# HGRN2 and dilated-attention block: the first projection's input is loaded a second time, turned by the host, and scaled in place

## The chip, the cores and the metric
The kernel runs on one core of one Trainium2 chip. The metric is the device time of one execution in microseconds (us). All times below are those of the kernel before the change, unless a text says otherwise.

## The reference
Everything is float32. `x` has 2048 tokens (rows) of 1024 features. Only the first lines matter here; the mixers that follow are unchanged.

```
u    = x * rsqrt(mean(x*x, axis=-1) + 1e-6) * norm_w      # one factor per token, one gain per feature
proj = u @ w_in                                          # 1024 x 4096
hg_q, hg_f, hg_i, hg_z, at_q, at_k, at_v, at_z = split(proj)
o_hg = per-head RMSNorm of an HGRN2 gated recurrence (4 heads), times silu(hg_z)
o_at = mix of three dilated causal window attentions (8 heads), times silu(at_z)
out  = rms_norm(x + concat(o_hg, o_at) @ w_out, final_norm_w)
```

## The kernel before
The program is written engine by engine; each engine runs its own instructions strictly in the order written, and semaphores order them across engines. The 2048 tokens are 16 **tiles** of 128 tokens. Every projection is made of three matmuls in a reduced-precision fp32 form: `u` and the weights are each split into a high and a low part (`u_hi`, `u_lo`, `w_hi`, `w_lo`), so that `u_hi`*`w_hi` + `u_hi`*`w_lo` + `u_lo`*`w_hi` is accumulated over the eight 128-feature slices (lines 665 to 667). The stages are: a **prologue** that makes `u_hi` and `u_lo` for all 16 tiles and, on the way, the values and gates of the first head from them; the HGRN2 heads; the attention units; the output projection and the last norm. `u_hi` and `u_lo` stay in SBUF for all the projections.

The matmul contracts over the partitions, so `u` must lie *turned*: features in the partitions, tokens along a row. `x` arrives with tokens in the partitions. In the prologue each tile t goes through this:

- SyncE loads the tile's 128 x 1024 floats of `x` into one of four slots `xt` (`load_x`, line 431), 0.5 MB each.
- ScalarE squares it and sums along the row (line 1106; signals `xsq_done`). GpSimd makes the token's inverse norm `rstd` of the sum, in two tiny instructions (lines 1321, 1325; `rstd_done`).
- VectorE multiplies the tile by `rstd`, one number per partition (line 1498; `xn_done`).
- TensorE turns the product in eight 128 x 128 transposes into two PSUM banks (`x_transposes`, line 699; `xT_done`).
- VectorE multiplies the two banks by the gains `norm_w` into a buffer `un` (line 1471, 128x512 twice; `un_done`).
- ScalarE copies `un` to `u_hi` (line 1101; `uhi_done`); VectorE subtracts to get `u_lo` (line 1471, 128x1024; `ulo_done`).
- TensorE runs the tile's 24 matmuls (`phase1_tile`, lines 665 to 667; `vz_ready`). ScalarE copies the result to `vg_tile` and takes a sigmoid of the gate half (lines 1091, 1092; `sig_done`). GpSimd multiplies twice (lines 1305, 1307; `gated`). SyncE stores the tile to DRAM (`phase1_store`, line 420).

In the order that is written out by hand, TensorE turns tile t+2 just before the matmuls of tile t, ScalarE squares tile s in its step s and handles the result of tile s-4 in the same step, and SyncE, in its step s, first stores tile s-5 and then loads tile s+4 of `x`. That load waits for `xn_done`, since line 1498 is the last reader of the slot. SyncE waits in this same order, so whatever stands behind a wait stands still with it:

```
for step in range(TILES + 5):
    if step >= 5:
        phase1_store(0, step - 5)
    if step - 3 in SPLIT_AT:
        load_piece(1, SPLIT_AT.index(step - 3))
    if step + X_SLOTS < TILES:
        after(xn_done, step + 1)
        load_x(step + X_SLOTS)
```

Four times in the prologue (after tiles 1, 4, 7 and 10, `SPLIT_AT`), a piece of the next weights is loaded and split too. TensorE runs 28 and then 12 idle transposes of the identity (line 706) before the first tiles are ready. After tile 15 the first `queries` (lines 665 to 667, now 128x512) wait for `sig_done` of tile 15.

Of the kernel before, what the change touches and what calls it, by code (L numbers as in the profile page):

```python
# [25 lines left out]
X_SLOTS = 4  # L26
Q_SLOTS = 3
# [103 lines left out]
def build(nc, x, w_groups, w_units, w_out, norm_w, gate_g, lb_logits, final_w, rope, near_mask, far_mask, tri_masks, out):  # L131
# [7 lines left out]
    with ExitStack() as ctx:  # L139
# [70 lines left out]
        ss, rstd = p2.take(TILES), p2.take(TILES)  # L210

# [80 lines left out]
        rstd_done, xn_done, xT_done = sem("rstd_done"), sem("xn_done"), sem("xT_done")  # L292
# [105 lines left out]
        def _(sp):  # L398
# [33 lines left out]

            load_x(0)
# [225 lines left out]
        def _(pe):  # L659
# [34 lines left out]
            def x_transposes(t):  # L694
                pe.wait_ge(xn_done, t + 1)
                if t >= 2:
                    pe.wait_ge(un_done, t - 1)
                for k in range(KT_N):
                    last = nc.tensor.transpose(bank[1 + 2 * (t % 2) + k // 4][:, (k % 4) * P:(k % 4 + 1) * P],
                                               xn[t % 2][:, k * P:(k + 1) * P], ident[:, :])  # L700
                last.then_inc(xT_done, 1)
# [6 lines left out]
            idle_transposes(28)  # L708
            x_transposes(0)
            idle_transposes(12)  # L710
            x_transposes(1)
# [1209 lines left out]
```

## Time and profile before

| | us |
|---|---|
| median of 3 runs | 1281.92 (1281.78 to 1283.44) |
| profiled execution, its own time | 1279.88 |
| its span in the profile | 1278.1 |
| TensorE matmuls busy | 1244.5 (97%) |
| VectorE busy | 704.9 (55%) |
| ScalarE busy | 461.2 (36%) |
| GpSimd busy | 434.4 (34%) |
| first matmul of tile 0 | 15.34 from the span's start |
| first matmul of the first `queries` (end of the prologue) | 80.32 |

In the rows further down, PE is TensorE, PEld its weight load, DVE VectorE, ACT ScalarE, POOL GpSimd and SP SyncE; SPq is SyncE issuing a DMA. A row of the order of time gives the start, how long it took, engine, line and operation, what is written and read, and how many instructions were merged; in brackets stands how long the engine had been idle, and what released it. `room` is the work area of SBUF in which `xt`, `xn`, `un`, `rstd` and others lie. Durations overlap a little in a pipelined engine, so where a step is costed the starts are compared.

### The profile page before, as it was taken

The page shows a single profiled execution, that of the slowest core. Times are in us where ns is not written, and L with a number is a line of the kernel's source. Part 1 is how long each engine was busy: PE and PEld are TensorE (multiplying, and loading weights), DVE is VectorE, ACT ScalarE, POOL GpSimd, SP SyncE. Part 2 cuts the span into 40 slices and gives each one's busy share as a digit, 9 for nine tenths or more (in the row PEclk, how much of TensorE's full clock was granted, in tenths as well). Part 3 has the DMA queues.
Part 4 walks back from the last instruction along what each step waited for, and adds up shares of the span by engine and source line. Part 5 has one row for each costly group of instructions (what it writes and reads, how often), then busy time and mean ns, then how long its engine had stood idle before and what let it go on. Part 6 is the DMA issues. An engine that isn't in the chain of part 4 may idle for free.

```text
span 1278.1 us, 24337 instructions
## 1 busy us (share of the span) xinstructions
PE 1244.5 (97%) x8944; PEld 1086.7 (85%) x8944; DVE 704.9 (55%) x1933; ACT 461.2 (36%) x1328; POOL 434.4 (34%) x441
## 2 busy tenths in 40 slices
PE   7999999999999999999999999999999998999997
PEld 6988989999999989999888888888888876888886
DVE  6837867887767797111455445545554455333232
ACT  6631222222222212112555455545554556421121
POOL 5543344243534413121243335334533334021000
PEclk9999999999999999999999999999999999999999
DMA  6520122211221222241455455545554666544431
GB/s 231 158 91 18 55 63 83 75 59 59 63 79 59 75 67 75 77 127 57 119 143 139 121 138 140 144 119 141 149 139 120 165 178 201 161 140 148 148 116 66
DMA packets 121717, 143.94 MB, mean 113 GB/s; under 512 B 20352, under 2 KB 86400, under 8 KB 121600
## 3 DMA queue, kind: packets, MB, share of 16 engines
q1 hardware_dynamic: 117024, 134.26, 37.1%
q10 hardware_dynamic: 4576, 8.13, 2.3%
q8 instruction: 72, 1.18, 0.4%
q14 instruction: 45, 0.37, 0.1%
HBM read 87.56 MB, written 29.62 MB: 92 GB/s over the span
## 4 chain that ended last, share of the span: by engine, by line
PE 56%; DMA 4%; DVE 2%; POOL 1%; ACT 1%; issue 1%; SPq 1%; POOLq 0%; ACTq 0%; DVEq 0%
PE bank L836 6%; PE bank L835 6%; PE bank L834 6%; PE bank L862 5%; PE bank L864 5%; PE bank L863 5%; PE bank L926 3%; PE bank L935 3%; PE bank L990 3%; PE bank L997 3%; PE bank L665 2%; PE bank L666 2%; PE bank L667 2%; PE bank L963 2%; PE bank L971 1%; PE bank L979 1%
## 5 line engine op out<-in xcount | busy, mean ns | idle before, releaser
L665 PE MATMUL bank<-w_hi,u_hi 128*128 128x256 f32 x768 | 220.8, 287 | 2.9 <-DVE u_lo L1471 2.4
L666 PE MATMUL bank<-w_lo,u_hi 128*128 128x256 f32 x768 | 217.9, 284 | 0.0
L667 PE MATMUL bank<-w_hi,u_lo 128*128 128x256 f32 x768 | 217.8, 284 | 0.0
L665 PEld LDWEIGHTS bank<-w_hi,u_hi 128*128 128x128 f32 x768 | 147.9, 193 | 4.6 <-DVE u_lo L1471 3.9
L666 PEld LDWEIGHTS bank<-w_lo,u_hi 128*128 128x128 f32 x768 | 147.9, 193 | 0.1
L667 PEld LDWEIGHTS bank<-w_hi,u_lo 128*128 128x128 f32 x768 | 147.8, 192 | 0.0
L1471 DVE TENSOR_TENSOR room<-room 128x256 f32<-128x256 f32 (+6 forms) x386 | 131.1, 387 | 16.6 <-POOL room L1356 10.7
L834 PE MATMUL bank<-u_hi,w_hi 128*128 128x512 f32 x256 | 107.8, 421 | 0.6 <-issue 0.5
L1471 DVE TENSOR_TENSOR t<-bank,tab 128x512 f32<-128x512 f32 x64 | 42.5, 684 | 118.2 <-DMA tab<-in_rope 53.5
L835 PE MATMUL bank<-u_lo,w_hi 128*128 128x512 f32 x256 | 101.9, 398 | 2.8 <-DMA far_v<-values 2.8
L1385 POOL TENSOR_TENSOR r<-t,t 64x512 f32<-64x512 f32 x16 | 35.0, 2187 | 199.6 <-DVE w L1758 188.8
L862 PE MATMUL bank<-u_hi,mT_hi 128*128 128x512 f32 x256 | 102.0, 398 | 0.7 <-DVE mT_lo L1471 0.6
L836 PE MATMUL bank<-u_hi,w_lo 128*128 128x512 f32 x256 | 102.0, 398 | 0.0
L665 PE MATMUL bank<-u_hi,w_hi 128*128 128x512 f32 x256 | 101.0, 395 | 0.6 <-ACT sg_tile L1092 0.6
L864 PE MATMUL bank<-u_hi,mT_lo 128*128 128x512 f32 x256 | 100.0, 391 | 0.0
L667 PE MATMUL bank<-u_hi,w_lo 128*128 128x512 f32 x256 | 99.8, 390 | 0.0
L863 PE MATMUL bank<-u_lo,mT_hi 128*128 128x512 f32 x256 | 99.8, 390 | 0.0
L666 PE MATMUL bank<-u_lo,w_hi 128*128 128x512 f32 x256 | 99.7, 390 | 0.0
L1186 ACT COPY pT<-bank 128x512 f32<-128x512 f32 x60 | 35.3, 588 | 130.3 <-PE bank L963 130.3
L1471 DVE TENSOR_TENSOR hh<-bank,xr 128x512 f32<-128x512 f32 x32 | 22.1, 690 | 107.0 <-PE bank L864 103.2
L935 PEld LDWEIGHTS bank<-ks,qd 128*128 128x128 f32 x256 | 78.5, 310 | 1.7
L935 PE MATMUL bank<-ks,qd 128*128 128x128 f32 (+3 forms) x256 | 79.8, 319 | 0.0
(169 smaller groups left out, 2840.9 us busy)
## 6 DMA issues: line engine op xcount, KB each, us to landing
qd<-turned SPq DMA_DIRECT2D x64, 256.0 KB, 4.5
stage<-in_w_groups SPq DMA_DIRECT2D x42, 256.0 KB, 4.0
room<-in_x SPq DMA_DIRECT2D x16, 512.0 KB, 4.0
values_gates<-vg_tile SPq DMA_DIRECT2D x64, 128.0 KB, 1.7
room<-values_gates SPq DMA_DIRECT2D x16, 512.0 KB, 3.9
tab<-in_rope SPq DMA_DIRECT2D x16, 512.0 KB, 4.4
wide<-mix_weights SPq DMA_DIRECT2D x32, 256.0 KB, 3.9
xr<-in_x SPq DMA_DIRECT2D x16, 512.0 KB, 4.8
```

Source lines behind the costliest of these rows:

```text
L665: yield nc.tensor.matmul(dst, lhs_hi(k), rhs_hi(k), start=(k == 0), stop=False)
L666: yield nc.tensor.matmul(dst, lhs_hi(k), rhs_lo(k), start=False, stop=False)
L667: last = nc.tensor.matmul(dst, lhs_lo(k), rhs_hi(k), start=False, stop=(k == KT_N - 1))
L834: yield nc.tensor.matmul(bk[:, :], wh[:, k, :], u_hi[:, k, sl], start=(k == 0), stop=False)
L835: yield nc.tensor.matmul(bk[:, :], wh[:, k, :], u_lo[:, k, sl], start=False, stop=False)
L836: last = nc.tensor.matmul(bk[:, :], wl[:, k, :], u_hi[:, k, sl], start=False, stop=(k == KT_N - 1))
L862: yield nc.tensor.matmul(bk[:, :], mT_hi[t % 2][:, k, :], wo_hi[half][:, k, :], start=(k == 0), stop=False)
L863: yield nc.tensor.matmul(bk[:, :], mT_hi[t % 2][:, k, :], wo_lo[half][:, k, :], start=False, stop=False)
L864: last = nc.tensor.matmul(bk[:, :], mT_lo[t % 2][:, k, :], wo_hi[half][:, k, :], start=False, stop=(k == KT_N - 1))
L926: last = nc.tensor.matmul(dst, q[h][:, z, j * P:(j + 1) * P], key_tiles(h, T), start=(z == 0), stop=(z == 1))
L935: last = nc.tensor.matmul(bank[2 + h][:, 0:P * (g + 1)], q[h][:, z, j::CH], keys, start=(z == 0), stop=(z == 1))
L1471: return nc.vector.tensor_tensor(dst, a_, b_, op)
```

## The change
The host gives `x` a second time as `x_turned`: for each tile, features in the partitions, tokens along the row. A tile of it goes straight to the buffer `xT`, which has three slots of two tiles each (a **pair**, 1 MB). The `x` in token order is still loaded, for the squares alone. TensorE no longer turns `x`; it turns a column of `rstd` that is broadcast along the row, one 128 x 128 transpose per tile, which leaves the 128 inverse norms in a row in every partition (`rstd_rows`). VectorE then makes `xT * norm_w * rstd` in place, one instruction per 128-feature slice for both tiles of a pair (`scaled`). Tiles 0 and 1 are handled one by one. `u_hi` and `u_lo` are made from `xT`. The order of the work is written anew on all engines. In the new file the lines are: `load_x` 438, `load_pair` 441, the single turned tiles 445 and 449, store 427, transposes of `rstd` 720, squares 1123, high parts 1127, result copy and sigmoid 1113 and 1114, inverse norms 1354 and 1357, gates 1337 and 1339, `scaled` 1530, low parts 1510.

```diff
+XT_SLOTS = 3
+PAIRS = TILES // 2
...
-        xn = [p2.take(D) for _ in range(2)]
+        xT = [p2.take(2, KT_N, P) for _ in range(XT_SLOTS)]
-        un = [p2.take(KT_N, P) for _ in range(2)]
...
+        def rstd_bank(t):
+            return bank[3 + t] if t < 2 else bank[1 + t // 2 % 2]
...
             load_x(0)
+            sp.dma_start(xT[0][:, 0], x_turned[0].rearrange("p (k c) -> p k c", k=KT_N)).then_inc(xT_first, 16)
             load_piece(0, 0)
             load_x(1)
             load_piece(0, 1)
+            sp.dma_start(xT[0][:, 1], x_turned[1].rearrange("p (k c) -> p k c", k=KT_N)).then_inc(xT_landed[0], 16)
...
             load_x(2)
             load_x(3)
+            load_pair(1)
+            load_pair(2)
...
-            for step in range(TILES + 5):
-                if step >= 5:
-                    phase1_store(0, step - 5)
-                if step - 3 in SPLIT_AT:
-                    load_piece(1, SPLIT_AT.index(step - 3))
-                if step + X_SLOTS < TILES:
-                    after(xn_done, step + 1)
-                    load_x(step + X_SLOTS)
+            for t in range(TILES):
+                if t + X_SLOTS < TILES:
+                    after(xsq_done, t + 1)
+                    load_x(t + X_SLOTS)
+                if t % 2 and t // 2 + XT_SLOTS < PAIRS:
+                    after(ulo_done, t + 1)
+                    load_pair(t // 2 + XT_SLOTS)
+                if t - 1 in SPLIT_AT:
+                    load_piece(1, SPLIT_AT.index(t - 1))
+                if t >= 1:
+                    phase1_store(0, t - 1)
+            phase1_store(0, TILES - 1)
...
-            def x_transposes(t):
...
+            def rstd_rows(t, many):
+                q = t // 2
+                pe.wait_ge(rstd_done, t + many)
+                if q >= 2:
+                    pe.wait_ge(un_done, 2 * (q - 1))
+                for z in range(t, t + many):
+                    last = nc.tensor.transpose(rstd_bank(z)[:, (z % 2) * P:(z % 2 + 1) * P],
+                                               rstd[:, z:z + 1].to_broadcast([P, P]), ident[:, :])
+                last.then_inc(rows_done, many)
...
             for t in range(TILES):
-                if 1 <= t < TILES - 2:
-                    x_transposes(t + 2)
+                if t % 2 and t // 2 + 2 < PAIRS:
+                    rstd_rows(t + 3, 2)
                 pe.wait_ge(ulo_done, t + 1)
                 matmuls = phase1_tile(0, t, "prologue")
                 if t == 0:
                     run(itertools.islice(matmuls, 16))
-                    x_transposes(2)
+                    rstd_rows(2, 2)
                 run(matmuls)
...
+            for t in range(1, TILES + 2):
+                if t < TILES:
+                    high_parts(t)
+                if t + 3 < TILES:
+                    square(t + 3)
...
+                if t >= 2:
+                    phase1_tile(0, t - 2, "prologue")
...
+            for t in range(1, TILES + 2):
+                if t % 2 == 0 and t + 3 < TILES:
+                    inverse_norms(t + 2, 2)
+                if t >= 2:
+                    phase1_tile(0, t - 2, "prologue")
...
+            def scaled(t, many):
...
+                dve.wait_ge(rows_done, t + many)
+                for k in range(KT_N):
+                    part = slot[:, first:first + many, k, :]
+                    last = nc.vector.scalar_tensor_tensor(out=part, in0=part, scalar=nw[:, k:k + 1],
+                                                          in1=rstd_bank(t)[:, first * P:(first + many) * P].rearrange("p (t c) -> p t c", t=many),
+                                                          op0=ALU.mult, op1=ALU.mult)
+                last.then_inc(un_done, many)
...
+            for q in range(1, PAIRS):
+                if q + 1 < PAIRS:
+                    scaled(2 * q + 2, 2)
+                low_parts(2 * q)
+                low_parts(2 * q + 1)
```

The diff doesn't show how far each load of `x` now stands from the stores and the squares. The rows below are the order in which the instructions stand on SyncE and on ScalarE (line, operation, written and read, partitions x elements, and what the row waits for). The first two fences are SyncE's queue from the point at which the first slots of `xt` are reused; `room<-in_x` is a load of `x`, `values_gates<-vg_tile_59` and `_60` are the stores of even and odd tiles, `stage` a weight piece. Before:

```order
L431 DMA room<-in_x 128x1024 [waits xn_done] x4
L410 DMA stage_56<-in_w_groups 128x512 [waits lo_done]
L431 DMA room<-in_x 128x1024 [waits xn_done]
L420 DMA values_gates<-vg_tile_59 128x256 [waits gated]
L431 DMA room<-in_x 128x1024 [waits xn_done]
L420 DMA values_gates<-vg_tile_60 128x256 [waits gated]
L431 DMA room<-in_x 128x1024 [waits xn_done]
L420 DMA values_gates<-vg_tile_59 128x256 [waits gated]
```

And now:

```order
L438 DMA room<-in_x 128x1024 [waits xsq_done] x2
L441 DMA room<-in_x_turned 128x2x1024 [waits ulo_done]
L427 DMA values_gates<-vg_tile_59 128x256 [waits gated]
L438 DMA room<-in_x 128x1024 [waits xsq_done]
L417 DMA stage_56<-in_w_groups 128x512 [waits lo_done]
L427 DMA values_gates<-vg_tile_60 128x256 [waits gated]
L438 DMA room<-in_x 128x1024 [waits xsq_done]
L441 DMA room<-in_x_turned 128x2x1024 [waits ulo_done]
```

Before, the loads of tiles 4 to 8 stand ahead of the store of tile 0; now only those of tiles 4 and 5 do, and from there on the load of tile n stands right behind the store of tile n-6, where before that of tile n stood ahead of the store of tile n-8.

The next two are ScalarE's queue from the result of tile 1 to that of tile 2 (`x_landed` is the landing of a load of `x`, `vz_ready` the end of a tile's matmuls). Before:

```order
L1091 COPY vg_tile_60<-bank 128x256 [waits vz_ready]
L1092 ACTIVATE sg_tile_62<-bank 128x128
L1076 CAST w_hi_52<-stage_56 128x512 [waits w_landed0]
L1101 CAST u_hi<-room 128x8x128 [waits un_done]
L1106 ACTIVATE room<-room 128x1024 [waits xsq_done,x_landed2]
L1091 COPY vg_tile_59<-bank 128x256 [waits vg_stored0,vz_ready]
L1092 ACTIVATE sg_tile_61<-bank 128x128
```

And now:

```order
L1113 COPY vg_tile_60<-bank 128x256 [waits vz_ready]
L1114 ACTIVATE sg_tile_62<-bank 128x128
L1098 CAST w_hi_52<-stage_56 128x512 [waits w_landed0]
L1127 CAST u_hi<-room 128x8x128 [waits un_done]
L1123 ACTIVATE room<-room 128x1024 [waits xsq_done,x_landed3]
L1113 COPY vg_tile_59<-bank 128x256 [waits vg_stored0,vz_ready]
L1114 ACTIVATE sg_tile_61<-bank 128x128
```

The square between the two results was that of tile 6 before, and is that of tile 7 now: while the result of tile n is copied just after the square of tile n+4 before, it now comes just after the square of tile n+5.

## Rows read from the trace of the kernel before

**Rows 1.** The page: busy share of TensorE in 40 slices of the span, in tenths.
```profile
PE   7999999999999999999999999999999998999997
```

**Rows 2.** Order of time, TensorE: transposes of `x`, and the last tile's end.
```profile
37.47 1.04 PE L699 MATMUL bank<-ident,room 128*128 128x128 f32 x8
38.26 0.36 PE L665 MATMUL bank<-w_hi,u_hi 128*128 128x256 f32 x1
...
41.09 0.28 PE L667 MATMUL bank<-w_hi,u_lo 128*128 128x256 f32 x1
...
70.02 1.03 PE L699 MATMUL bank<-ident,room 128*128 128x128 f32 x8
...
80.32 0.50 PE L665 MATMUL bank<-u_hi,w_hi 128*128 128x512 f32 x1 [0.64 <-ACT sg_tile L1092]
```

**Rows 3.** Order of time, VectorE, 26 to 29 us.
```profile
26.16 1.29 DVE L1471 TENSOR_TENSOR room<-bank,nw 128x512 f32<-128x512 f32 x2 [0.92 <-PE bank L699]
27.37 0.74 DVE L1498 TENSOR_SCALAR room<-room 128x1024 f32<-128x1024 f32 x1
28.03 1.43 DVE L1471 TENSOR_TENSOR u_lo<-room,u_hi 128x1024 fp32r<-128x1024 f32 x1
```

**Rows 4.** Whole run by line and shape, VectorE (count, busy us, mean ns).
```profile
L1657 DVE SCALAR_TENSOR_TENSOR room<-room,bank 128x128 f32<-128x128 f32 x60 | 20.9, 348 | 2.7 <-PE bank L768 0.7
L1813 DVE SCALAR_TENSOR_TENSOR gate<-gate,bank 128x512 f32<-128x512 f32 x15 | 10.3, 687 | 41.8 <-ACT gate L1257 41.8
```

**Rows 5.** Busy by stretch: us, PE, clock granted to it, DMA share, GB/s.
```profile
0.00:8.00 8.00, 4.66 (x27) 1.00 0.54 153
8.00:16.00 8.00, 4.47 (x36) 1.00 1.04 400
...
488.00:491.00 3.00, 0.59 (x16) 1.00 0.27 84
...
492.00:495.00 3.00, 3.00 (x16) 0.50 0.46 143
```

**Rows 6.** Order of time, ScalarE: square, result of a tile, table load.
```profile
22.66 1.28 ACT L1092 ACT_TABLE_LOAD   x1
...
27.48 1.05 ACT L1101 CAST u_hi<-room 128x1024 fp32r<-128x1024 f32 x1 [0.32 <-DVE room L1471]
28.44 1.05 ACT L1106 ACTIVATE room<-room 128x1024 f32<-128x1024 f32 x1
29.40 0.18 ACT L1106 ACTIVATION_READ_ACCUMULATOR room<-room 128x1 f32 x1
29.49 0.35 ACT L1091 COPY vg_tile<-bank 128x256 f32<-128x256 f32 x1
...
70.48 0.28 ACT L1092 ACTIVATE sg_tile<-bank 128x128 f32<-128x128 f32 x1
```

**Rows 7.** Order of time, GpSimd: inverse norm of a tile, gates of another.
```profile
22.48 0.19 POOL L1321 TENSOR_SCALAR room<-room 128x1 f32<-128x1 f32 x1 [2.72 <-ACT room L1106]
22.75 0.55 POOL L1325 TENSOR_TENSOR room<-room 128x1 f32<-128x1 f32 x1
...
70.84 0.46 POOL L1305 TENSOR_TENSOR vg_tile<-vg_tile,sg_tile 128x128 f32<-128x128 f32 x1 [2.25 <-ACT sg_tile L1092]
71.38 0.41 POOL L1307 TENSOR_TENSOR vg_tile<-vg_tile,room 128x128 f32<-128x128 f32 x1
```

**Rows 8.** Order of time, SyncE: DMA issues.
```profile
45.29 0.43 SPq L420 DMA_DIRECT2D values_gates<-vg_tile  x1
45.77 0.43 SPq L410 DMA_DIRECT2D stage<-in_w_groups  x1
...
71.82 4.07 SPq L420 DMA_DIRECT2D values_gates<-vg_tile  x2
```

**Rows 9.** One line's instructions: the loads of `x` issued from 30 to 60 us.
```profile
L431 SPq DMA_DIRECT2D room<-in_x x6: 327/328/328, 33.3 to 52.7; - x6
...
DMA to landing us min/median/max: 3.6/3.7/5.3
```

More of the change, by code:

```diff
@@ L291, in build @@
         x_landed0, x_landed1, xsq_done = sem("x_landed0"), sem("x_landed1"), sem("xsq_done")
-        rstd_done, xn_done, xT_done = sem("rstd_done"), sem("xn_done"), sem("xT_done")
+        rstd_done, rows_done = sem("rstd_done"), sem("rows_done")
+        xT_first, xT_landed = sem("xT_first"), [sem(f"xT_landed{i}") for i in range(XT_SLOTS)]
         un_done, uhi_done, ulo_done = sem("un_done"), sem("uhi_done"), sem("ulo_done")
@@ L692, in _ @@
             pe.sem_inc(lev_mm, LEVELS)
-            def x_transposes(t):
[L695 to L701, printed above, removed]
+            def rstd_rows(t, many):
[7 more added lines that the diff above has]
+                last.then_inc(rows_done, many)
             def idle_transposes(many):
@@ L1317, in _, with inverse_norms @@
             own = 2
-            for step in range(TILES + 4):
-                if step < TILES:
-                    pool.wait_ge(xsq_done, step + 1)
-                    nc.gpsimd.tensor_scalar(ss[:, step:step + 1], ss[:, step:step + 1], 1.0 / D, EPS,
-                                            ALU.mult, ALU.add).then_inc(pool_step, 1)
-                    own += 1
-                    pool.wait_ge(pool_step, own)
-                    nc.gpsimd.tensor_tensor(rstd[:, step:step + 1], ss[:, step:step + 1], half_neg[:, 0:1],
-                                            ALU.pow).then_inc(rstd_done, 1)
-                if step < 3:
-                    for i in ((0,), (1, 2), (3,))[step]:
-                        split_lo(0, i, 0)
-                if step == 3:
-                    pool.wait_ge(g_landed, 16)
-                    nc.gpsimd.tensor_copy(g_cur, g_all[:, 0, :]).then_inc(pool_step, 1)
-                    own += 1
-                if step >= 4:
-                    phase1_tile(0, step - 4, "prologue")
+            def inverse_norms(t, many):
+                nonlocal own
+                pool.wait_ge(xsq_done, t + many)
+                nc.gpsimd.tensor_scalar(ss[:, t:t + many], ss[:, t:t + many], 1.0 / D, EPS, ALU.mult, ALU.add).then_inc(pool_step, 1)
+                own += 1
+                pool.wait_ge(pool_step, own)
+                nc.gpsimd.tensor_tensor(rstd[:, t:t + many], ss[:, t:t + many], half_neg[:, 0:many], ALU.pow).then_inc(rstd_done, many)
+            inverse_norms(0, 1)
+            split_lo(0, 0, 0)
+            inverse_norms(1, 1)
+            split_lo(0, 1, 0)
+            inverse_norms(2, 2)
+            split_lo(0, 2, 0)
+            split_lo(0, 3, 0)
+            pool.wait_ge(g_landed, 16)
+            nc.gpsimd.tensor_copy(g_cur, g_all[:, 0, :]).then_inc(pool_step, 1)
+            own += 1
+            pool.wait_ge(pool_step, own)
+            for t in range(1, TILES + 2):
[3 more added lines that the diff above has]
+                    phase1_tile(0, t - 2, "prologue")
             pool.wait_ge(lb_ready, 1)
@@ L1476, in low_parts @@
                 dve.wait_ge(uhi_done, t + 1)
[L1477 removed]
+                tt(u_lo[:, :, t * P:(t + 1) * P], xT[t // 2 % XT_SLOTS][:, t % 2], u_hi[:, :, t * P:(t + 1) * P].bitcast(F32),
                    ALU.subtract).then_inc(ulo_done, 1)
[L1480 to L1509 removed]
@@ new lines, in scaled @@
+            def scaled(t, many):
+                q = t // 2
+                first, slot = t % 2, xT[q % XT_SLOTS]
+                if t == 0:
+                    dve.wait_ge(xT_first, 16)
+                else:
+                    dve.wait_ge(xT_landed[q % XT_SLOTS], 16 * (q // XT_SLOTS + 1))
+                dve.wait_ge(rows_done, t + many)
[5 more added lines that the diff above has]
+                last.then_inc(un_done, many)
@@ new lines, in _ @@
+            dve.wait_ge(const_ready, 17)
+            scaled(0, 1)
+            low_parts(0)
+            scaled(1, 1)
+            scaled(2, 2)
+            low_parts(1)
+            dve.wait_ge(lb_landed, 16)
+            nc.vector.tensor_tensor(lb_tmp, lb_in[:, 0, :], lb_in[:, 1, :], ALU.max).then_inc(lb_step, 1)
+            dve.wait_ge(lb_step, 1)
+            nc.vector.tensor_tensor(lb_in, lb_in, lb_tmp[:, None, :].to_broadcast([P, 2, HG_UNITS]),
+                                    ALU.subtract).then_inc(lb_step, 1)
```

80 lines of the change are left out of this document (29 added, 51 removed).

## The prediction
> **What bounds the kernel now.** I read the busy shares of the slices first [rows 1]: TensorE is at nine tenths or more in every slice but the first, the last and one of eight tenths, so time won or lost on its path in one stage reaches the end of the kernel almost whole. The change is confined to the prologue, so I then read that stage in order of time, engine by engine. TensorE's rows [rows 2] show a tile there: eight transposes take 0.8 us (37.47 to 38.26) and 24 matmuls 2.95 us (38.26 to 41.09, plus the 0.12 us step of one). That is 3.75 us; from 37.47 to 70.02 there are eight tiles, 4.07 us each, so about 0.3 us a tile is waiting, and VectorE is what TensorE waits for. VectorE spends, from start to start, 1.21 us on the gains, 0.66 on the inverse norm and 1.2 to 1.4 on the low part [rows 3], some 3.2 us a tile, in a chain with TensorE's transposes. The prologue ends when the first queries start, at 80.32 us [rows 2]. I measure the change there.
>
> **What goes, engine by engine.** TensorE loses 16 x 8 transposes, 16 x 0.8 = 12.8 us, and gets 16 single ones of 0.1 us, 1.6 us: 11 us less. VectorE loses 0.66 + 1.21 us a tile and gets eight two-operand instructions of 128x256 for a pair. The trace has none of this shape; the nearest take 0.35 us with 128 elements and 0.69 us with 512 [rows 4]. Two additions or multiplications of 128x512 start 0.6 us apart [rows 3], so 256 elements should take 0.34 us (bounds 0.27 and 0.6), eight of them 2.7 us (2.2 to 4.8). With two low parts a pair then costs VectorE 5.2 us instead of 6.4. GpSimd makes two norms in one go. By itself all of this is a gain.
>
> **What is added: a chain through the loads.** The order rows ahead of this text are the point. SyncE now loads tile n of x only behind the store of tile n-6, and that store waits until GpSimd has gated the tile. ScalarE, in turn, copies the result of tile n-5 only after it has squared tile n. So from tile 6 on there is a ring with one load in it: result of tile n-6, its gates, its store, load of tile n, square of tile n, result of tile n-5, and so on. Before, the load of tile n stood ahead of the store of tile n-8, three tiles earlier than its square needed it, so its landing time was hidden. Now nothing hides it. One turn of the ring, from starts to starts:
> - the copy, 0.25 us (29.49 to 29.74), and the sigmoid, 0.28 [rows 6];
> - 0.08 us to GpSimd and 0.95 for its two gates, 70.84 to 71.79 [rows 6, 7];
> - 0.03 us to SyncE's store, and 0.48 from one issue to the next [rows 8];
> - the load: 3.6 to 5.3 us from issue to landing, median 3.7 [rows 9]. I take 3.9, for a 128 KB store is now issued just ahead of it;
> - 0.05 us to ScalarE and 1.05 for the square, 28.44 to 29.49 [rows 6].
>
> The sum is 7.07 us a tile, against 4.07 now. After each odd square GpSimd first makes the pair's norms, 0.82 us [rows 7], which holds the gates back by 0.35 us: four times. ScalarE's high part (0.96 us) and the weight splits lie inside the wait for the load.
>
> By the Trainium skill, DMA: Bandwidth & Descriptors, "Anatomy of one DMA", a transfer costs about 2.0 us and its bytes at 436 GB/s; the page gives it for DMAs issued by GpSimd. For 0.5 MB that is an estimate of 3.2 us, and ten turns would cost 7 us less than in my sum. The loads of this trace (median 3.7 us) say the page's figure is too short here.
>
> **The start.** Ahead of and with the load of tile 4 there are now 7.3 MB in SyncE's queue: x of tiles 0 to 4 (2.6), turned tiles 0 to 5 (3.1), weights (1.05), the small tables (0.5). The trace moved 1.22 MB in the first 8 us and 0.40 MB per us when saturated [rows 5], so the last byte is there at 8 + 6.1 / 0.40 = 23.3 us, the signal at about 24.2, tile 5 at 25.5. ScalarE squares tile 4 (to 25.3), makes the high part of tile 2 (26.2), squares tile 5 (27.3), and only then copies the result of tile 0, with a table load of 1.28 us [rows 6]: 29.2 us. Gates and store put the first load of the ring (tile 6) at 30.7 us; its square ends at 35.7.
>
> **The sum.** Nine more turns, 9 x 7.07 + 4 x 0.35 = 65.0 us, end the square of tile 15 at 100.7 us. TensorE waits for the norms of tiles 14 and 15 before tile 11: 0.9 us of GpSimd, 0.2 of transposes, so tile 11 starts at 101.8. Then the scaling (2.7) and the low part (1.2) allow tile 12 at about 105.9. TensorE has by then idled some 6 us in each pair. In a later stage an idle stretch of about 2 us (488 to 491 us, 0.59 us busy) is followed by three whole microseconds at half clock, 1.2 GHz, at a granted clock of 0.50 [rows 5]. I give tile 11 four microseconds at the lower level: 17 of its matmuls at 0.24 us, the others at 0.12, to 106.7 us. Tiles 12 to 15 take 4 x 2.9 = 11.6, to 118.3, and the queries come 0.8 us later as now: 119.1 us. Against 80.3 that is **+38.8 us**. In the ring itself the low clock costs nothing: tile pairs at half clock take 2 x 5.8 us of the 14.5 us that two turns last. VectorE isn't on the ring either: 5.2 us of 14.5. The extra 8.4 MB, once the queue of the start has drained, share some 2.4 MB per 14.5 us, 0.17 MB per us of the 0.40. After the prologue nothing is changed, and TensorE's slices are full, so the delay stays. Against the profiled execution of 1279.9 us this gives 1318.7; the median stood 2.0 us above that execution, so I predict 1320.7.
>
> The Trainium skill, TensorE: Matmul & The Clock Gate, "HAM oscillation", says that bursts of matmuls split by long waits each begin at 1.2 GHz; the row at 492 us agrees with its 0.50.
>
> **Rivals.**
> - *The ring turns slower.* The turned pairs (1 MB each) share the queues with x. If every load took the longest 5.3 us [rows 9], ten loads would add 14 us: +53, 1334.7 us. Against it: a pair is issued behind x, not ahead, and has 7 us to drain before the next load.
> - *Loads are not on the path; VectorE and TensorE take turns.* The scaling of a pair waits for the transposes of `rstd`, which TensorE issues after the matmuls of tile 2q-2, and stands ahead of the low part of tile 2q. A pair then takes 2.95 + 0.3 + 2.7 + 1.2 + 0.1 = 7.3 us. Tile 2 would start near 32.3 (norms of tiles 4 and 5 at 28.1, then 4.2 us), tile 12 five pairs later at 68.8, the queries after 4 tiles and 0.8 us at 81.2: +0.9, no change. It needs the loads to arrive 4 us or more earlier than the queue lets them go.
> - *Faster: TensorE becomes the only bound of the prologue.* If scaled tiles were always ready, a tile would take 2.95 + 0.1 instead of 4.07 us; over tiles 2 to 15 that is 14.3 us won, and the late start costs 5 (tile 2 at 31 instead of 26, which is 38.3 less three tiles of 4.07): -9, 1272.6 us. This decides if scaling and square run at least one pair ahead of the matmuls, so if the wait for the rstd transposes and the ring are both shorter than two tiles of matmuls, 5.9 us. The ring's two turns are 14.5, so I hardly believe it.
> - *The change doesn't do what it says*, if the load didn't wait behind the store. But the order rows show SyncE's waits in one queue, so this falls together with the two cases above.
>
> **How the numbers follow.** My forecast has 0.86 (with its own unknowns), the slower ring 0.06, the no-change case 0.04, the faster one 0.04. In the forecast the landing (3.6 to 4.7 over ten loads: -3 to +8), the queue of the start (-3 to +3), the clock and the scaling in the tail (-1 to +3) leave 1311 to 1334 us, which also takes in most of the slower ring. A measurement of this kernel tells about 0.2%, 2.6 us, from no change. Slower by over 0.2%: 0.92; within: 0.04; faster: 0.04.
>
> **What would show it.** Right: loads of x between 30 and 100 us issued about 7 us apart, each directly behind a store; ScalarE's largest wait is a DMA into `room`, some 4 us ten times; TensorE idle for 6 us or more before every other tile, released by GpSimd's `rstd`, its granted clock below 1 there; VectorE's scaling near 0.34 us an instruction; the first 128x512 queries near 119 us; the later stages as long as before. Wrong: loads issued 4 us apart, a VectorE busy throughout the prologue, queries before 90 us, or a later stage that gives the time back.

## The result and the profile after

The changed kernel took 1321.01 us, the median of four runs (1315.72 to 1323.79); the kernel before took 1281.94 beside it (four runs, 1281.78 to 1283.44). The ratio is 1.0308, with a 95% interval of 1.0289 to 1.0326: **slower by 39 us**, where 1320.7 us was predicted. The profiled execution took 1320.39 us with a span of 1318.6. The rows below come from it.

SyncE in order of time, where [rows 8] show the same loads before:
```profile
30.02 0.33 SPq L427 DMA_DIRECT2D values_gates<-vg_tile  x1
30.39 0.43 SPq L438 DMA_DIRECT2D room<-in_x  x1
...
37.21 0.33 SPq L427 DMA_DIRECT2D values_gates<-vg_tile  x1
37.58 0.43 SPq L438 DMA_DIRECT2D room<-in_x  x1
38.05 0.46 SPq L441 DMA_DIRECT2D room<-in_x_turned  x1
44.86 0.33 SPq L427 DMA_DIRECT2D values_gates<-vg_tile  x1
45.23 0.43 SPq L438 DMA_DIRECT2D room<-in_x  x1
...
94.89 0.33 SPq L427 DMA_DIRECT2D values_gates<-vg_tile  x1
95.27 0.43 SPq L438 DMA_DIRECT2D room<-in_x  x1
```
Each load of `x` starts 0.37 us behind the start of a store. From 30.39 to 95.27 us there are nine turns, 64.88 us, 7.21 each. How long the loads of L438 took between 28 and 100 us, as [rows 9] had it:
```profile
DMA to landing us min/median/max: 3.6/3.7/4.4
```

One turn on ScalarE, then on GpSimd, in order of time [rows 6, 7]:
```profile
41.65 1.06 ACT L1123 ACTIVATE room<-room 128x1024 f32<-128x1024 f32 x1 [4.04 <-DMA room<-in_x]
...
42.71 0.35 ACT L1113 COPY vg_tile<-bank 128x256 f32<-128x256 f32 x1
42.96 0.28 ACT L1114 ACTIVATE sg_tile<-bank 128x128 f32<-128x128 f32 x1
```
```profile
42.88 0.19 POOL L1354 TENSOR_SCALAR room<-room 128x2 f32<-128x2 f32 x1 [4.48 <-ACT room L1123]
43.22 0.70 POOL L1357 TENSOR_TENSOR room<-room 128x2 f32<-128x2 f32 x1
43.88 0.46 POOL L1337 TENSOR_TENSOR vg_tile<-vg_tile,sg_tile 128x128 f32<-128x128 f32 x1
44.42 0.41 POOL L1339 TENSOR_TENSOR vg_tile<-vg_tile,room 128x128 f32<-128x128 f32 x1
```
This is a turn with a pair's norms in it. The load is issued at 37.58, the square starts at 41.65 (+4.07), the copy at 42.71 (+1.06), the sigmoid at 42.96 (+0.25), the first gate at 43.88 (+0.92, behind the pair's norms), the store at 44.86 (+0.98) and the next load at 45.23 (+0.37): 7.65 us. That is the whole turn, with no gap left over. In the summary of waits, 20 to 110 us for ScalarE and 20 to 120 us for TensorE (total us, times, longest), the ring's load is ScalarE's largest row. TensorE's idle time comes of it: 5.6 to 6.9 us ahead of every other tile, until GpSimd's norms are there:
```profile
ACT room L1123 <- DMA room<-in_x: 46.9, 11, 4.9
```
```profile
PE bank L720 <- POOL room L1357: 36.2, 6, 6.9
PE bank L684 <- POOL w_lo L1324: 3.4, 1, 3.4
```

TensorE in order of time [rows 2]: the start of tiles 3 and 11, the end of the lower clock in tile 11, and the first queries:
```profile
43.98 0.69 PE L720 MATMUL bank<-ident,room 128*128 128x128 f32 x2 [6.89 <-POOL room L1357]
44.31 0.56 PE L684 MATMUL bank<-w_hi,u_hi 128*128 128x256 f32 x1
...
101.28 0.69 PE L720 MATMUL bank<-ident,room 128*128 128x128 f32 x2 [5.61 <-POOL room L1357]
101.63 0.56 PE L684 MATMUL bank<-w_hi,u_hi 128*128 128x256 f32 x1
...
105.83 0.33 PE L685 MATMUL bank<-w_lo,u_hi 128*128 128x256 f32 x1
...
118.89 0.50 PE L684 MATMUL bank<-u_hi,w_hi 128*128 128x512 f32 x1 [0.64 <-ACT sg_tile L1114]
```
VectorE in order of time [rows 3], a pair's scaling and its two low parts:
```profile
44.77 3.22 DVE L1530 SCALAR_TENSOR_TENSOR room<-room,nw,bank 128x256 f32<-128x256 f32 x8 [10.20 <-PE bank L720]
47.91 2.35 DVE L1510 TENSOR_TENSOR u_lo<-room,u_hi 128x1024 fp32r<-128x1024 f32 x2
```
Busy time by stretch [rows 5], and the page's slices [rows 1]:
```profile
44.00:48.00 4.00, 4.00 (x19) 4.00 (x20) 3.23 (x9) 0.17 (x1) 0.75 (x2) 0.51 0.51 156
48.00:52.00 4.00, 3.82 (x32) 3.62 (x31) 3.17 (x7) 2.53 (x5) 0.92 (x2) 1.00 0.02 8
```
```profile
PE   5659999999999999999999999999999998999997
```
In the stretches, the clock granted to TensorE is the number behind the five engines: 0.51, its lower level of 1.2 GHz, from 44 to 48 us, after 6.89 us of idle time, and 1.00, the level of 2.4 GHz, from 48 to 52. The loss is in the first three digits of the slices. The first queries start at 118.89 us, 38.6 later than at 80.32; what follows them takes 1199.7 us of the span against 1197.8. In the profiled executions of the twelve kernels below, that rest took 1193.7 to 1206.4 us, though none of them changes it: the 1.9 us are within what one execution differs from another. So the experiments are compared by the start of the first queries as well as by their times.

### The profile page after: what moved, and what is told of

It reads as the page before. It is cut to its first block, busy times and chain, and to the rows that moved or that the text cites. A ratio compares the mean times of both kernels' runs of the same rounds, so it can differ in the third digit from the quotient of the medians.

```text
span 1318.6 us, 24120 instructions
## 1 busy us (share of the span) xinstructions
PE 1247.7 (95%) x8836; PEld 1088.2 (83%) x8836; DVE 692.9 (53%) x1957; ACT 460.1 (35%) x1328; POOL 426.4 (32%) x427
## 4 chain that ended last, share of the span: by engine, by line
PE 51%; DMA 5%; DVE 2%; SPq 1%; POOL 1%; issue 1%; ACT 1%; ACTq 0%; POOLq 0%; DVEq 0%
PE bank L856 5%; PE bank L858 5%; PE bank L857 5%; PE bank L884 5%; PE bank L886 4%; PE bank L885 4%; PE bank L948 3%; PE bank L957 2%; PE bank L1012 2%; PE bank L1019 2%; PE bank L684 2%; PE bank L686 2%; PE bank L685 2%; PE bank L985 2%; DMA attended<-wide 1%; PE bank L993 1%
## 5 line engine op out<-in xcount | busy, mean ns | idle before, releaser
L684 PE MATMUL bank<-w_hi,u_hi 128*128 128x256 f32 x768 | 226.3, 295 | 5.0 <-POOL w_lo L1324 3.8
L685 PE MATMUL bank<-w_lo,u_hi 128*128 128x256 f32 x768 | 222.9, 290 | 0.0
L686 PE MATMUL bank<-w_hi,u_lo 128*128 128x256 f32 x768 | 222.6, 290 | 0.0
L684 PEld LDWEIGHTS bank<-w_hi,u_hi 128*128 128x128 f32 x768 | 153.5, 200 | 6.5 <-POOL w_lo L1324 4.5
L685 PEld LDWEIGHTS bank<-w_lo,u_hi 128*128 128x128 f32 x768 | 153.5, 200 | 0.1
L686 PEld LDWEIGHTS bank<-w_hi,u_lo 128*128 128x128 f32 x768 | 153.0, 199 | 0.0
L1510 DVE TENSOR_TENSOR room<-room 128x256 f32<-128x256 f32 (+6 forms) x386 | 128.3, 379 | 16.6 <-POOL room L1395 10.3
L858 PE MATMUL bank<-u_hi,w_lo 128*128 128x512 f32 x256 | 101.8, 397 | 0.0
L1208 ACT ACTIVATE p_near<-p_near,st_near 128x256 f32<-128x256 f32 (+1 forms) x128 | 63.3, 496 | 42.6 <-DVE st_near L1769 36.9
```

The lines of the kernel that those rows point to most:

```text
L684: yield nc.tensor.matmul(dst, lhs_hi(k), rhs_hi(k), start=(k == 0), stop=False)
L685: yield nc.tensor.matmul(dst, lhs_hi(k), rhs_lo(k), start=False, stop=False)
L686: last = nc.tensor.matmul(dst, lhs_lo(k), rhs_hi(k), start=False, stop=(k == KT_N - 1))
L858: last = nc.tensor.matmul(bk[:, :], wl[:, k, :], u_hi[:, k, sl], start=False, stop=(k == KT_N - 1))
L1208: nc.scalar.activation(buf, buf, ACT.Exp, scale=-1.0, bias=stt[:, j, h:h + 1], accum_out=stt[:, j, 2 + h:3 + h]).then_inc(e_done, 1)
L1510: return nc.vector.tensor_tensor(dst, a_, b_, op)
```

## Experiments

**The theory (ring):** a load of `x` waits in SyncE's queue behind a store, the store waits for GpSimd and ScalarE, and ScalarE waits for an earlier load. **Rivals:** the doubled traffic; the turns that VectorE's scaling and TensorE take; TensorE's clock. All runs had the kernel before beside them, at 1280.0 to 1281.9 us.

**1. The store one tile later.** A turn of the ring then covers two tiles.
```
-                if t >= 1:
-                    phase1_store(0, t - 1)
+                if t >= 2:
+                    phase1_store(0, t - 2)
+            phase1_store(0, TILES - 2)
```


> Only the place of the stores in SyncE's queue changes: in step t it now stores tile t-2 instead of t-1, so each load of x stands behind one store less. Ring theory (the loads of x wait for a store, the store for a result, the result for the square of the tile loaded before): one turn of the ring, about 7.2 us plus one tile's work of ScalarE (2.6 us), now serves two tiles, some 4.9 us a tile instead of 7.2; ten turns less about 2.3 us and an earlier first one: 25 to 30 us faster than the changed kernel, about 1293 us. Volume theory (8.4 MB more on the DMA queues is what holds the prologue up): no change, 1321 us, since the bytes are the same. Turn-taking theory (scaling a pair on VectorE between the transposes of rstd and the low parts sets the pair's time): no change either.

Measured: 1296.43 us (four runs, 1293.55 to 1301.36), ratio to before 1.0115 (1.0089 to 1.0141). The first queries start at 93.16. A move of the stores that saves no work gives back 25 of 39 us. ScalarE still waits for `x`, less (20 to 120 us):
```profile
ACT room L1124 <- DMA room<-in_x: 17.2, 8, 4.7
```

**2. The turned pair ahead of `x`.** Loads and their waits change places in odd steps.
```
+                if t % 2 and t // 2 + XT_SLOTS < PAIRS:
+                    after(ulo_done, t + 1)
+                    load_pair(t // 2 + XT_SLOTS)
                 if t + X_SLOTS < TILES:
                     after(xsq_done, t + 1)
                     load_x(t + X_SLOTS)
```


> In each odd step SyncE issues the 1 MB turned pair ahead of the 0.5 MB load of x instead of behind it. Ring theory: the load's landing is in the ring, and on four turns it now has 1 MB ahead of it, 2.6 us at 400 GB/s; at the start the load of tile 5 also waits for the low part of tile 1, some 5 us. Together 14 to 17 us slower than the changed kernel, about 1336 us. Volume theory: the same bytes, within 3 us of 1321. Turn-taking theory: no change.

Measured: 1345.53 us (one run), 24.5 more than the changed kernel. The queries start at 138.35, 19.5 later than in it, where 14 to 17 us were expected; the other 5 us lie behind the prologue, which the edit doesn't touch, so they belong to this one execution. In the prologue the ring theory is right in direction and some 3 to 5 us too low. In each of the four turns whose load was issued behind a pair, 9.7 to 10.3 us passed from that load to the next, as here:
```profile
79.83 0.50 SPq L438 DMA_DIRECT2D room<-in_x  x1
89.78 0.33 SPq L427 DMA_DIRECT2D values_gates<-vg_tile  x1
90.15 1.41 SPq L438 DMA_DIRECT2D room<-in_x  x1
```

**3. The result ahead of the square on ScalarE.** This opens the ring at its other joint.
```
-                if t + 3 < TILES:
-                    square(t + 3)
...
                     phase1_tile(0, t - 2, "prologue")
+                if t + 3 < TILES:
+                    square(t + 3)
```


> ScalarE alone is changed: in each step of the prologue it handles the result of tile t-2 first and squares tile t+3 after it, instead of the other way round; SyncE's queue stays. Ring theory: the result no longer waits for the square of the same step, which takes one link out of the ring; the next one is longer (the square waits one result more), so 6 to 12 us faster than the changed kernel, about 1312 us. Volume and turn-taking theories: no change, 1321 us.

Measured: 1326.54 us (one run), queries at 123.98: **a miss**. Waits for `x` did fall, from 46.9 us to 12.5, but waits for a tile's result took their place. ScalarE, 20 to 120 us:
```profile
ACT vg_tile L1113 <- PE bank L686: 39.2, 11, 6.2
ACT room L1123 <- DMA room<-in_x: 12.5, 4, 4.7
```
The transposes of `rstd` at 62.46, 76.81 and 90.94 us lie 14.35 and 14.13 us apart, as long as two turns of the ring. The rows between the first two show why. ScalarE in order of time:
```profile
68.00 0.37 ACT L1113 COPY vg_tile<-bank 128x256 f32<-128x256 f32 x1 [5.78 <-PE bank L686]
...
74.49 1.06 ACT L1123 ACTIVATE room<-room 128x1024 f32<-128x1024 f32 x1 [3.07 <-DMA room<-in_x]
```
The transposes at 62.46 let TensorE run a tile at the lower clock, its result is copied at 68.00, its store goes out at 69.61 and the load behind it at 69.98, the square starts at 74.49, the norms at 75.72, and the next transposes at 76.81. The load still stands behind a store; the way back now leads through TensorE's matmuls instead of through ScalarE's order. Every link of this second cycle was in the changed kernel already. There the copy at 49.97 came 5.99 us after the transposes at 43.98, held by the square and not by the matmuls, which had ended 1.0 us earlier, so the cycle was hidden just under the ring. I had broken one cycle and met another of the same length. The edit also put the splits of the weight pieces ahead of the squares: at 59.62 ScalarE had waited 5.67 us for a piece to land, and that pair took 17.8 us (44.67 to 62.46), where the changed kernel's took 14.0 (43.98 to 58.00). Those 3.8 us are most of the 5.1 by which the queries come later.

**4. Half the turned traffic taken away.** Pairs 3 to 7 are not loaded, so tiles 6 to 15 are made from the pairs already there and the result is not that of the reference; every engine's work stays.
```
-                if t % 2 and t // 2 + XT_SLOTS < PAIRS:
-                    after(ulo_done, t + 1)
-                    load_pair(t // 2 + XT_SLOTS)
...
-                    dve.wait_ge(xT_landed[q % XT_SLOTS], 16 * (q // XT_SLOTS + 1))
+                    dve.wait_ge(xT_landed[q % XT_SLOTS], 16)
```


> The turned pairs 3 to 7 are not loaded; the slots keep what was scaled in them before, so the input of tiles 6 to 15 is not that of the reference. 5.2 MB less on the DMA queues. Ring theory: each load of x lands perhaps 0.1 to 0.2 us sooner, 1 to 3 us in all, about 1319 us. Volume theory: most of the loss goes, 15 to 35 us faster, 1290 to 1305 us. Turn-taking theory: no change.

Measured: 1324.62 us (one run), queries at 119.50, landings 3.4/3.8/4.8. 5.2 MB less on the queues and no gain: the volume is not the cause.

**5. Stores and pairs behind the loads.** SyncE's loop gets back nearly the distance that the kernel before had from load to store: the load of tile n stands behind the store of tile n-8, where before it was n-9. The square, the copy and all work stay.
```
+            for t in range(TILES + 3):
...
+                if t >= 3:
+                    phase1_store(0, t - 3)
+                if t % 2 == 0 and 2 <= t and t // 2 - 1 + XT_SLOTS < PAIRS:
+                    after(ulo_done, t)
+                    load_pair(t // 2 - 1 + XT_SLOTS)
```


> SyncE's queue alone: in step t it loads x of tile t+4, then a weight piece, then stores tile t-3, then loads a turned pair one step later than before. No load of x stands behind a store that it could be waiting for. Ring theory: the ring is gone; the loads of x land before their squares, and the prologue is bound by what was hidden under it, VectorE and TensorE taking turns: transposes of rstd, 3.2 us of scaling, 1.2 of low part, 2.9 of matmuls, some 7.7 us a pair. First queries at about 85 us (before: 80.3, changed: 118.9), so about 1287 us, 34 us faster than the changed kernel and still 4 or 5 slower than before. Volume theory: the loss stays, over 1310 us, since the bytes are the same.

Measured: 1290.27 us (nine runs, 1284.91 to 1294.23), ratio 1.0066 (1.0042 to 1.0091), queries at 89.36. Thirty-one of the 39 us are gone; 34 were expected. The landings grew; L438 from 24 to 115 us:
```profile
DMA to landing us min/median/max: 4.7/6.3/8.3
```
TensorE's waits, 20 to 90 us, are now split between VectorE's low part and the norms:
```profile
PE bank L683 <- DVE u_lo L1509: 8.5, 6, 1.7
PE bank L719 <- POOL room L1356: 8.0, 3, 5.3
```

**6. The low part ahead of the next pair's scaling,** on top of 5.
```
+                low_parts(2 * q)
                 if q + 1 < PAIRS:
                     scaled(2 * q + 2, 2)
-                low_parts(2 * q)
```


> As e5, and on VectorE the low part of tile 2q stands ahead of the scaling of the next pair instead of behind it, so that TensorE can start tile 2q while VectorE scales. If the turn-taking is what bounds e5, a pair goes from 7.7 us towards the 6.0 us of its matmuls and rstd transposes: first queries near 80 or 81 us, about 1283 us, 4 to 5 us faster than e5. If it isn't, no change against e5.

Measured: 1289.39 us (ten runs, 1285.12 to 1292.53), ratio 1.0064 (1.0044 to 1.0084), queries at 87.69. Against 5 this is no clear difference, where 4 to 5 us were expected: what was saved at the low part was paid at the norms, for which TensorE now waited 15.0 us instead of 8.0.

**7. The start reordered,** on top of 6: `x` of tiles 4 and 5 is loaded ahead of the second pair, the last two pieces of the first weights ahead of turned tile 1, and ScalarE and GpSimd split them before the next squares and norms.
```
+            for t in range(2):
+                after(xsq_done, t + 1)
+                load_x(t + X_SLOTS)
             load_pair(2)
...
-            square(2)
-            square(3)
             split_hi(0, 2, 0)
             split_hi(0, 3, 0)
+            square(2)
+            square(3)
```


> As e6, and the start is ordered anew: x of tiles 4 and 5 is loaded ahead of the second turned pair, the first weights ahead of turned tile 1, and ScalarE and GpSimd split the last two pieces of the first weights before the squares of tiles 2 and 3. It should take 2 to 4 us off the start: first queries at 77 to 79 us, about 1280 us, 1 to 3 us faster than the kernel before, if nothing else steps in. If the start is bound by the sum of the bytes (7 MB at 400 GB/s) and not by their order, no change against e6.

Measured: 1288.06 us (twelve runs, 1285.55 to 1292.93), ratio 1.0052 (1.0033 to 1.0071), queries at 86.36: no clear difference against 6, and not the 1280 us hoped for. The transposes of `rstd` at 37.58, 45.47 and 53.27 us show 7.8 to 7.9 us a pair (8.5 to 9.1 in the next two), and GpSimd's norms end the wait ahead of them. From 45.47 the way leads through no store: the tile's matmuls, the copy of its result at 48.81, the next high part at 49.32, the square at 50.75 (behind 0.38 us of waiting for `x`), the norms at 52.18, the transposes at 53.27.

**8 and 9. The clock held up.** Forty idle transposes stand ahead of each pair's rstd transposes, in the changed kernel (8) and in 3 (9).
```
                 if t % 2 and t // 2 + 2 < PAIRS:
+                    idle_transposes(40)
                     rstd_rows(t + 3, 2)
```


> The changed kernel with 40 idle transposes of the identity (4.7 us) ahead of the rstd transposes of every pair from tile 4 on, inside the waits of 6 us and more. The granted clock should stay at 2.4 GHz in the ring. If, as forecast, the low clock costs nothing in the ring and about 1 us in the tail, 1319 to 1321 us. If TensorE at half clock is on the chain, 2 us a pair come back, some 10 us: about 1310.

> ScalarE as in e3 (result of tile t-2 before the square of tile t+3), and 40 idle transposes (4.7 us) ahead of the rstd transposes of each pair from tile 4 on, as in e8. In e3 ScalarE waited 39 us for matmuls to end, so there the matmuls lie on the chain. If e3 missed its gain because TensorE ran at half clock behind each long wait, about 2 us a pair come back: 8 to 12 us faster than e3, about 1316 us. If the clock has no part in it, e3's time, 1324 to 1327 us, or a little more where the idle transposes outlast the wait.

Measured, 8: 1321.74 us (four runs, 1320.86 to 1322.79), queries at 120.71. The granted clock from 30 to 100 us, first in the changed kernel, then in 8:
```profile
30.00:100.00 70.00, 40.38 (x244) 38.97 (x242) 27.44 (x53) 25.52 (x50) 15.05 (x29) 0.74 0.51 169
```
```profile
30.00:100.00 70.00, 56.61 (x433) 54.76 (x433) 27.31 (x53) 24.53 (x49) 15.28 (x30) 0.91 0.48 164
```
From 0.74 to 0.91, and no time won: in the ring the low clock costs nothing, as the prediction said. Measured, 9: 1321.61 us (four runs, 1319.31 to 1323.73), 4.9 less than the one run of 3, and queries at 120.43 instead of 123.98, 3.5 earlier. Both are well short of the 8 to 12 us expected. Matmuls at the higher clock did bring the copy 3.34 us behind the transposes (74.63 to 77.97) instead of 5.54, but then GpSimd's gates ran into VectorE's low parts (78.31 to 80.67):
```profile
78.60 2.38 POOL L1338 TENSOR_TENSOR vg_tile<-vg_tile,sg_tile 128x128 f32<-128x128 f32 x1 [3.12 <-ACT sg_tile L1115]
```
In 3 the same gate, at 68.63, took 0.46 us. So of the 2.2 us won at the matmuls 1.9 were lost again at this gate, and as much at 47.51 (2.40) and 92.47 (2.39).

**10. Squares a tile further ahead,** on top of 7: ScalarE squares tile t+4 in step t, and GpSimd makes the norms a tile sooner.
```
-                if t + 3 < TILES:
-                    square(t + 3)
+                if t != 2 and t + 4 < TILES:
+                    square(t + 4)
```


> As e7, and ScalarE squares tile t+4 instead of t+3 in step t, GpSimd makes a pair's norms one tile earlier, and those of tiles 4 and 5 ahead of the copy of the gate gains. In e7 a pair took 7.8 us: the end of a tile's matmuls, its copy on ScalarE, a high part, the square of the other tile, the norms, the rstd transposes, which stand ahead of the next tile's matmuls. If that chain is what is left, it leaves the path: some 6.3 us a pair instead of 7.8 and 2 to 4 us at the start, first queries at 74 to 78 us against 86.4, about 1278 us, 2 to 6 us faster than the kernel before. If something else holds the pair (the 5.7 us of VectorE with GpSimd's port contention, or the landing of x), 1283 to 1288 us.

Measured: 1295.82 us (six runs, 1291.37 to 1299.73), ratio 1.0118 (1.0097 to 1.0139), queries at 94.09: **a second miss**, where about 1278 us were expected. A square that comes earlier in ScalarE's order stands ahead of older results, and so shortens the distance round the ring. ScalarE's waits from 16 to 120 us have the ring's row again:
```profile
ACT room L1125 <- DMA room<-in_x: 27.3, 8, 6.3
```

**11. The loads well ahead,** on top of 10: stores, pieces and pairs two steps later.
```
-                if t >= 3:
-                    phase1_store(0, t - 3)
+                if t >= 5:
+                    phase1_store(0, t - 5)
```


> As e10, and SyncE's queue follows the time at which things fall due: in step t it loads x of tile t+4, then a weight piece (two steps later than in e10), then stores tile t-5 (was t-3), then loads a pair one step later. Nothing else changes. Ring theory: in e10, where ScalarE squares one tile further ahead, the ring closed again (27 us of waits of ScalarE for x, first queries at 94 us); with the stores two steps further back it is open, pairs take 6 to 6.5 us, first queries at 73 to 78 us, about 1275 us, 18 us faster than e10 and 3 to 7 us faster than the kernel before. If squares ahead are bad for another reason, e10's time, 1293 to 1298 us.

Measured: 1279.30 us (twelve runs, 1274.79 to 1286.6) beside 1281.76 (17 runs), ratio 0.9984 (0.9966 to 1.0003), queries at 77.24, 3.1 us sooner than before the change. The ring's wait fell from 27.3 us (16 to 120 us, in 10) to 2.7 (16 to 78 us). As a kernel it can't be told from the one before, and the 1275 us expected were not reached. This takes the start, VectorE's order, the squares and SyncE's queue all changed; how much of the 3.1 us is the change's own gain is not shown, since the kernel before was not given the same orders.

**12. The ring put into the kernel before.** No turned copy, no pairs, the old scaling. Only SyncE's loop changes: the store of tile s-1 stands ahead of the load of tile s+4, and the weight pieces go out three steps earlier.
```
-            for step in range(TILES + 5):
-                if step >= 5:
-                    phase1_store(0, step - 5)
-                if step - 3 in SPLIT_AT:
-                    load_piece(1, SPLIT_AT.index(step - 3))
+            for step in range(TILES + 1):
+                if step in SPLIT_AT:
+                    load_piece(1, SPLIT_AT.index(step))
+                if step >= 1:
+                    phase1_store(0, step - 1)
```


> The kernel before, with only SyncE's loop changed: in step s it stores tile s-1 (was s-5) ahead of the load of tile s+4, and the weight pieces come earlier so that nothing deadlocks. x is loaded once and turned by TensorE as before; no turned copy, no scaling in place. Ring theory: a ring like that of the changed kernel, with one load of x, 7.3 us a tile from tile 5 on (copy and sigmoid 0.53, waits and gates 1.4, store ahead 0.4, load 3.9, square 1.05): the square of tile 15 ends near 104 us, the first queries come near 116 us instead of 80, about 1318 us, 36 us slower than the kernel before. Theories that lay the loss on the turned copy, on VectorE's scaling or on the added bytes: no change, 1282 us.

Measured: 1323.44 us (four runs, 1320.99 to 1323.92), ratio 1.0316 (1.0295 to 1.0337), queries at 120.65. SyncE in order of time, and ScalarE's waits from 20 to 120 us:
```profile
64.24 0.33 SPq L420 DMA_DIRECT2D values_gates<-vg_tile  x1
64.61 0.43 SPq L431 DMA_DIRECT2D room<-in_x  x1
...
71.80 0.33 SPq L420 DMA_DIRECT2D values_gates<-vg_tile  x1
72.17 0.43 SPq L431 DMA_DIRECT2D room<-in_x  x1
```
```profile
ACT room L1106 <- DMA room<-in_x: 54.2, 11, 5.6
```
About 36 us were expected. The order of SyncE's DMAs alone costs a kernel with none of the rest of the change 42 us, as much as the whole change did. This settles it.

## Why the prediction was right

**The forecast's mechanism held.** Loads are issued behind stores and 7.2 us apart, and taking that order away or putting it in moves the time by most of the loss or all of it (runs 1, 5 and 12).

**One count orders the kernels with a ring.** Follow a load back through SyncE's and ScalarE's order to the load that it depends on, and count the tiles between. A turn takes 7 us or more, so that count decides:

| tiles a turn | kernels | first queries at, us |
|---|---|---|
| 1 | changed, 4, 8, 12 (and 2, with a pair ahead of `x`) | 118.9, 119.5, 120.7, 120.7 (138.4) |
| 2 | 1, 10 (and 3, 9, on another cycle) | 93.2, 94.1 (124.0, 120.4) |
| 3 | 5, 6, 7 | 89.4, 87.7, 86.4 |
| 4 | 11 | 77.2 |
| 5 | before | 80.3 |

In the changed kernel, for instance, the load of n stands behind the store of n-6, and the result of n-6 behind the square of n-1: one tile. Before the change a tile took 4.07 us, so a turn over two tiles may last 8.1 us without a loss. A turn of 7.2 us would fit; with the landing grown from 3.7 us to 5.6 (run 1) it is some 9 us and doesn't. From three tiles on the count no longer decides: 5, 6 and 7 differ with the same count, and the kernel before, with the longest distance, is 3.1 us behind run 11.

**The steps.** The turn was put at 7.07 us, with 0.35 more in four turns. The five turns without norms took 6.64 to 7.19, mean 6.81; the four with norms 7.28 to 7.99, mean 7.71. The plain turn was put too long (store to load 0.37 us instead of 0.48, landing 3.7 instead of 3.9), the norms too short (they hold the gates back by 0.56 us, 0.92 less the usual 0.36; and from the load's issue to the square these turns took 3.70 to 4.42 us, the plain ones behind the first 3.63 to 3.75). The pair's own load, issued just behind `x` in them, is not shown to be the reason: in run 4, without these pairs, the same turns took 3.80 to 4.02 and the others, behind the first, 3.42 to 3.79. Nine turns came to 64.88 us against 65.0 because these errors cancel: the mechanism was right, and that the sum came so close is luck.

**The start.** The first load of the ring was put at 30.7 us and came at 30.39, by the queue's bytes and 0.40 MB per us; the trace moved 399 and 400 GB/s from 8 to 24 us.

**The scaling.** 0.39 us an instruction (3.14 us from the start of eight to the low part), not 0.34: 3.1 us a pair instead of 2.7. In the ring VectorE has 10.2 us to spare, so this counts only in the tail.

**The tail.** The square of tile 15 was to end at 100.7 us and ended at 100.0; the norms and transposes behind it took 1.6 us instead of 1.1, so tile 11, put at 101.8, started at 101.63. The lower clock level of 1.2 GHz lasted to about 105.9: 4.3 us of it, 4 predicted, though at 0.21 us a matmul, not 0.24. Queries: 119.1 predicted, 118.89 measured. Here too two small errors cancel. The bounds named for the terms add up to 1314 to 1335 us, the range stated was 1311 to 1334; nothing hangs on it here.

**The rivals.** The slower ring did not come; run 2 shows what it needs, a pair ahead of `x`. The doubled volume is ruled out by run 4, and by run 12, which has the loss without the volume; the low clock by run 8. The no-change case was the next bound, with too low a price: with loads off the path it gave queries at 81.2 us and 7.3 us a pair, and run 5 showed 89.4 and 8.0 or more. It was not the only bound there: run 6 took its wait for the low part away and won nothing clear. The faster case (71.3 us) stayed out of reach even in run 11, which needed four orders changed. That the loss is the ring is shown by runs 1, 4, 5, 8 and 12.

**What stays open.** What holds runs 5 to 7 at 86 to 89 us is shown only in part. In run 7 it is the way through ScalarE's order told above. In run 5 ScalarE still waited 1.5 and 2.0 us for `x` ahead of the squares at 52.02 and 61.65. GpSimd, slowed beside VectorE (below), adds to it: one of run 7's seven pair norms took 1.48 us instead of 0.70, none of run 5's did, but one gate in each pair of run 5 took 2.4 us instead of 0.46 (at 41.58, 49.62, 58.30 and 67.94), and the store behind it went out that much later. No run takes that away alone.

The order of issue decides because a DMA's wait is made on the issuing engine, as SyncE's rows show, where each load follows its store by 0.37 us and never goes ahead of it. The Trainium skill, DMA: Bandwidth & Descriptors, "Anatomy of one DMA", says so in a section on DMAs issued by GpSimd, of any wait for a semaphore: it happens on the issuing sequencer, before dispatch. Runs 5 and 12, with DMAs issued by SyncE, agree: -31 and +42 us for an order alone.

## What to carry to other kernels

Before counting what a change saves, draw the cycle that in-order queues close: for each load, what stands ahead of it, what that waits for, and how many tiles lie between it and the load it comes back to. The turn's latency divided by that count must be below the work of a tile; here 7.2 us over one tile, against 4.07, undid a saving on two engines. An instruction moved earlier on one engine can shorten that count (run 10) as a store moved forward on another does, and a broken cycle may have a twin that it hid (run 3). In an in-order queue whatever is moved ahead takes its own waits along: in run 3 the split of a weight piece held a square back by 5.67 us.

## What the runs showed of the hardware

**GpSimd stalls beside VectorE's low part.** GpSimd's pair norm takes 0.70 us in the changed kernel (43.22 us). In run 7 it took 1.48, and in the first of these fences VectorE, in the second GpSimd, in order of time:
```profile
43.64 1.22 DVE L1512 TENSOR_TENSOR u_lo<-room,u_hi 128x1024 fp32r<-128x1024 f32 x1
...
49.21 2.62 DVE L1512 TENSOR_TENSOR u_lo<-room,u_hi 128x1024 fp32r<-128x1024 f32 x2
```
```profile
43.93 1.48 POOL L1359 TENSOR_TENSOR room<-room 128x2 f32<-128x2 f32 x1
...
49.44 1.30 POOL L1339 TENSOR_TENSOR vg_tile<-vg_tile,sg_tile 128x128 f32<-128x128 f32 x1 [1.86 <-ACT sg_tile L1116]
50.82 1.27 POOL L1341 TENSOR_TENSOR vg_tile<-vg_tile,room 128x128 f32<-128x128 f32 x1
...
53.18 0.46 POOL L1339 TENSOR_TENSOR vg_tile<-vg_tile,sg_tile 128x128 f32<-128x128 f32 x1
53.71 0.41 POOL L1341 TENSOR_TENSOR vg_tile<-vg_tile,room 128x128 f32<-128x128 f32 x1
```
The norm started at 43.93, inside the low part that ends at 44.86, and ended 0.55 us after it; the two gates beside the next low parts took 1.30 and 1.27 us, without them 0.46 and 0.41. The Trainium skill, SBUF — State Buffer, "Who interferes with whom", says that a VectorE instruction with two SBUF inputs contends with a GpSimd instruction that reads SBUF, for ports that they share. The rows agree: low part, norm and gates are all of this kind. In run 9 the same gate took 2.38 us. In the ring the gates fall into VectorE's idle time and take 0.46 (43.88 us).

**A 0.5 MB load is not one number.** With one load at a time in the ring it lands in 3.7 us in the median (3.6 to 4.4), and in 3.8 without the pairs (run 4, 3.4 to 4.8). Where loads are issued ahead, among pairs, stores and pieces, the medians are 5.6 to 6.5 (runs 1 and 5 to 7), and 7.5 in run 11 (all from 24 to 115 us), where ScalarE waited only 2.7 us for them.
